# Routing and experts in one stage, with the blocks taken from both ends of the expert order

## The chip, the cores and the metric

The kernel runs on one core of one Trainium2 chip. The metric is the device time of one execution in microseconds (us). Three executions of the kernel before took 3208.84, 3212.40 and 3218.40 us; the median is 3212.4 us.

## The reference

Two transformer blocks follow each other, on 1024 tokens of width 1024 (S and D), in float32. Each ends with a mixture of experts: 16 experts in the first block, 32 in the second, in 4 groups. For every token:

```
grp    = argmax(group_logits)                 # 1 of 4 groups
e_in   = expert_logits[grp]                   # 4 or 8 logits of that group
top2   = top_k(e_in, 2)
weight = softmax(group_logits)[grp] * softmax over the two chosen
y      = sum over the two: weight * (silu(x @ w_gate[e]) * (x @ w_up[e])) @ w_down[e]
```

w_gate and w_up of an expert are 1024 x 256, w_down is 256 x 1024: 3 MB per expert. Everything ahead of the experts (projections, convolution or recurrence, attention, the output projection and the router's logits) is not touched.

## The kernel before

The program is a row of stages. Each stage owns its memory and semaphores, and `stage` clears the semaphores and makes all engines meet (line 116) when it ends. Within a stage each engine has its own instruction stream and its own queue; the engines meet at semaphores. `Steps` (called `own`) makes an engine wait for its own last instruction before it goes on. DMAs come from the queue of SP (weights, rows of the end) and from that of POOL (gathers and scatters by a list of rows).

`moe` (line 2423) runs two stages for each transformer block:

1. `route_tokens` (line 1402). VectorE (DVE) finds the group and the two experts of each token by comparisons over [128 tokens, 8 tiles, experts] tables. TensorE counts tokens by two products, one with a strict triangle (rank within a tile) and one with ones (totals). VectorE lays the experts' tokens out in blocks of 128, each block of one expert, and builds one-hot tables of place in the block and of block; 16 TensorE products turn them into a list of tokens per block (lines 1464, 1526 to 1563). Results are `token`, `choice`, `weights`, `expert` (of each block) and `passes`.
2. `run_experts` (line 1567 on). It walks the blocks in pairs p = 0, 1; `passes` says how often. SP reads the expert of a block from `expert` and loads its weights in three parts j = 0, 1 (1 MB each, halves of w_gate and w_up) and 2 (1 MB, w_down) into `raw[p][j]` (lines 1639 to 1651). ACT rounds them to a high part (`round_up`, `round_down`), VectorE subtracts to get the low part (`rest`, line 1867); each product is then three matmuls (high by high, high by low, low by high). POOL gathers the block's rows of v into `x[p]` (line 1679), TensorE turns them (line 1727), ACT and VectorE split them into `xT_high` and `xT_low`. TensorE makes the up products in two halves (line 1741), ACT and VectorE the gated middle, TensorE the down products (line 134), ACT copies them, and POOL scatters them (line 1691). At the end all rows are added up with their weights (line 1916).

A part's memory is given free one by one: SP loads `raw[p][j]` again once its low part is made; ACT rounds again once the products that read the high part are done. SP's loads, POOL's gathers and each engine's steps are in a fixed order written by hand. Before the loop ("first") the order of TensorE is: turn of block 0, turn of block 1, both up halves of block 0. In the list of blocks, slot n is block n. The experts of slots 0 and 1 are known to SP only from `expert`.

## Time and profile before

| | |
|---|---|
| median of 3 executions | 3212.4 us |
| profiled execution | 3206.69 us, span 3205.0 us |
| busy in the span | TensorE 85%, VectorE 49%, ACT 34%, POOL 25% |
| DMA | 405.00 MB, mean 126 GB/s |
| first expert part (routing, loop, end) | from about 1046 us |
| second expert part | from about 2753 us to the end |

The profile is of one execution. Busy time of an engine is the sum of its instructions; TensorE's clock is given as the granted share of full speed (0.50 or 1.00 within short stretches). Times in the rows are us from the start of the span.

### The profile page before, as it was taken

How to read it: one execution, taken by the hardware profiler on the slowest of the kernel's cores; microseconds unless marked ns; L12 is line 12 of the kernel's file. 1: busy time of each engine (PE TensorE's matmuls, PEld its weight loads, DVE VectorE, ACT ScalarE, POOL GpSimd, SP SyncE). 2: the span in 40 equal slices, each digit the busy share in tenths (PEclk: the TensorE clock that was granted, in tenths of full speed). 3: DMA queues.
4: the chain of work that ended last, by engine and by line, in shares of the span. 5: the costliest groups of instructions: out<-in, count | busy, mean ns of one | idle time of the engine just before them, and what ended most of it. 6: DMA issues, size and time to landing. Idle time of an engine off the chain costs nothing. (4 is left out here: it accounts for less than half of the span.)

```text
span 3205.0 us, 34426 instructions
## 1 busy us (share of the span) xinstructions
PE 2713.2 (85%) x11986; PEld 2022.5 (63%) x11986; DVE 1571.7 (49%) x1875; ACT 1085.8 (34%) x1435; POOL 798.1 (25%) x719
## 2 busy tenths in 40 slices
PE   5898897999979599719899699988999979499994
PEld 3897555767758477617655355556767757477773
DVE  4294341222232678661166444433643563487776
ACT  3012331000011377530133344431332131177773
POOL 1232331221211134302000233313322312034442
PEclk8999798999989699959799799998999989699997
DMA  2110112111132599853222232322111113299998
GB/s 88 34 46 24 31 33 55 53 39 39 33 119 99 215 345 361 324 187 129 114 59 60 69 78 78 80 53 68 40 39 46 46 49 144 110 345 335 343 326 323
DMA packets 237637, 405.00 MB, mean 126 GB/s; under 512 B 43512, under 2 KB 162632, under 8 KB 229608
## 3 DMA queue, kind: packets, MB, share of 16 engines
q1 hardware_dynamic: 220264, 370.21, 34.8%
q0 software_dynamic: 17280, 33.59, 2.7%
q8 instruction: 53, 0.87, 0.1%
q14 instruction: 40, 0.33, 0.0%
HBM read 351.97 MB, written 76.68 MB: 134 GB/s over the span
## 5 line engine op out<-in xcount | busy, mean ns | idle before, releaser
L1867 DVE TENSOR_TENSOR moe_run_w_low<-moe_run_w,moe_run_w_high 128x2048 fp32r<-128x2048 f32 x174 | 397.2, 2285 | 119.1 <-ACT moe_run_w_high L1793 108.9
L1793 ACT CAST moe_run_w_high<-moe_run_w 128x2048 fp32r<-128x2048 f32 x116 | 221.2, 1909 | 145.0 <-DMA moe_run_w<-w_up 66.4
L134 PE MATMUL rnn_ps<-uT_again_high,rnn_w_high 128*128 128x512 f32 x512 | 205.2, 401 | 36.1 <-POOL rnn_w_low L147 20.0
L134 PE MATMUL rnn_ps<-uT_again_low,rnn_w_high 128*128 128x512 f32 x512 | 202.5, 396 | 0.0
L134 PE MATMUL rnn_ps<-uT_again_high,rnn_w_low 128*128 128x512 f32 x512 | 202.3, 395 | 0.0
L1741 PE MATMUL moe_run_up<-moe_run_w_high,moe_run_xT_high 128*128 128x512 f32 x464 | 190.4, 410 | 0.3 <-DVE moe_run_w_low L1867 0.3
L134 PE MATMUL merge_gates<-uT_high,merge_wg_high 128*128 128x512 f32 x384 | 170.8, 445 | 17.4 <-POOL merge_wg_low L147 17.4
L1741 PE MATMUL moe_run_up<-moe_run_w_low,moe_run_xT_high 128*128 128x512 f32 x464 | 184.5, 398 | 0.0
L1741 PE MATMUL moe_run_up<-moe_run_w_high,moe_run_xT_low 128*128 128x512 f32 x464 | 184.3, 397 | 0.0
L1200 DVE TENSOR_TENSOR merge_gated<-merge_branch,merge_gate 128x512 f32<-128x512 f32 x48 | 33.2, 691 | 303.9 <-ACT merge_gate L1185 303.9
L1048 ACT ACTIVATE mla_probs<-mla_scores 128x512 f32<-128x512 f32 x192 | 94.2, 490 | 194.2 <-PE mla_scores L985 139.1
L1076 DVE TENSOR_REDUCE mla_piece_max<-mla_max 128x1 f32<-128x512 f32 (+1 forms) x192 | 100.7, 553 | 110.0 <-PE mla_max L960 71.0
L998 PE MATMUL mla_out<-mla_probs,mla_v 128*65 128x512 f32 (+3 forms) x384 | 153.6, 496 | 0.0
L134 PE MATMUL merge_gates<-uT_low,merge_wg_high 128*128 128x512 f32 x384 | 152.8, 398 | 0.0
L134 PE MATMUL merge_gates<-uT_high,merge_wg_low 128*128 128x512 f32 x384 | 151.6, 395 | 0.0
L1185 ACT ACTIVATE merge_gate<-merge_gates 128x512 f32<-128x512 f32 x48 | 28.8, 600 | 353.9 <-PE merge_branch L122 353.9
L134 PE MATMUL moe_run_down<-moe_run_w_high,moe_run_hT_high 128*128 128x512 f32 x232 | 99.2, 428 | 48.1 <-issue 44.7
L122 PE MATMUL mla_scores<-mla_q_hi,mla_k_hi 97*128 97x512 f32 x192 | 119.6, 623 | 23.0 <-DMA mla_q_hi<-mla_neg_rows 23.0
L134 PEld LDWEIGHTS rnn_ps<-uT_again_high,rnn_w_high 128*128 128x128 f32 x512 | 98.4, 192 | 59.0 <-issue 21.2
L122 PE MATMUL qkv_acc<-qkv_wq,latents_then_oT 128*128 128x512 f32 x288 | 126.9, 600 | 0.0
L1688 POOL COPY moe_run_to<-moe_choice 128x1 uint32 x58 | 64.6, 1114 | 243.9 <-ACT moe_run_y L1825 243.9
L122 PE MATMUL merge_branch<-features,merge_wy 128*128 128x512 f32 x256 | 117.7, 592 | 0.0
(447 smaller groups left out, 6722.2 us busy)
## 6 DMA issues: line engine op xcount, KB each, us to landing
moe_run_w<-exp_w SPq DMA_DIRECT2D x96, 512.0 KB
moe_run_w<-w_gate SPq DMA_DIRECT2D x68, 512.0 KB
moe_run_w<-w_up SPq DMA_DIRECT2D x68, 512.0 KB
moe_run_w<-w_down SPq DMA_DIRECT2D x34, 1024.0 KB
moe_run_w<-exp_w SPq DMA_DIRECT2D x24, 1024.0 KB
rnn_raw<-w_in SPq DMA_DIRECT2D x32, 512.0 KB
merge_raw<-w_in SPq DMA_DIRECT2D x24, 512.0 KB
moe_run_w_high<-moe_y SPq DMA_DIRECT2D x24, 512.0 KB, 8.0
```

What stands on the lines that cost most here:

```text
L122: last = pe.matmul(out, lhsT, rhs, start=(n == 0), stop=(n == len(pairs) - 1))
L134: last = pe.matmul(out, a, b, start=(k == 0), stop=(k == n - 1))
L998: pe.matmul(ps_o[n][0:DH + 1, first - a:b - a], v_aug[h % 2][0:rows, t, :], probs[g % R_P][0:rows, first - a:b - a], start=(t == 0), stop= ...
L1048: act.activation(probs[g % R_P][0:rows, first - a:b - a], ps_s[g % R_S][0:rows, first - a:b - a], ACT.Exp).then_inc(s_exp, 1)
L1076: dve.tensor_reduce(pm[:, i, n:n + 1], ps_m[g % R_M][:, 0:b - a], AX.X, ALU.max).then_inc(s_mxfree, 1)
L1185: act.activation(sg[u % NB][:], ps_g[u % NB][:], ACT.Sigmoid).then_inc(s_sg, 1)
L1200: dve.tensor_tensor(pr[b][:], ps_y[b][:], sg[b][:], ALU.mult).then_inc(s_done, 1)
L1688: pool.tensor_copy(to[p][:], r["choice"][:, bass.ds(b, 1)]).then_inc(s_to, 1)
L1741: last = pe.matmul(up[p][:], a, w, start=(h == 0 and k == 0), stop=(h == 1 and k == 3 * HK - 1))
L1793: act.copy(hi[p][j][:], raw[p][j][:]).then_inc(s_hi[j], 1)
L1867: dve.tensor_tensor(lo[p][j][:], raw[p][j][:], hi[p][j][:].bitcast(F32), ALU.subtract).then_inc(s_lo[j], 1)
```

## The change

`route_tokens` is gone and its steps are part of `run_experts`. In the new stage:

- A block's slot is no longer its number. With B blocks and half = B/2 rounded up, the block b < half has slot 2b, the others have slot 2B - 1 - 2b. Slot 0 is the first block of expert 0, slot 1 the last block of the last expert. So that this holds, every expert gets at least one block.
- SP loads the weights of expert 0 and of the last expert at the begin of the stage, by constants, and then waits for `expert`.
- ACT rounds five of these six parts ahead of the rest; POOL makes the first two low parts (`s_pre`), VectorE the others after the lists.
- POOL makes the tables' casts and clears x, and gathers the first two blocks' rows straight by `token`.
- The routing steps on VectorE are fewer and partly wider (both choices at once); the expert of each slot is found on one partition per slot and turned by a product. The weights' steps come after the loop.
- TensorE's order at the start is: turn of block 0, both up halves of block 0, turn of block 1.
- The routing's tables share memory with `g`, `squares` and `xT[1]`.

Core of the diff (declarations and the old routing, which the listing above shows, are left out):

```diff
+                def load(p, j, e):
+                    if j < 2:
+                        for n, w in enumerate(ups):
+                            sp.dma_start(raw[p][j][:, n], w[:, e, HK * j:HK * (j + 1), :]
+                                         .rearrange("p a c n -> p (a c) n")).then_inc(s_raw[p][j], 16)
+                    else:
+                        sp.dma_start(raw[p][j][:], dn[:, e].rearrange("p a c n -> p (a c) n")).then_inc(s_raw[p][j], 16)
+                def expert_of(i, p):
+                    return bass.ds(sp.value_load(expert[0:1, bass.ds(2 * i + p, 1)], min_val=0, max_val=E - 1), 1)
+                for p in range(2):
                     for j in range(3):
-                        if not first:
-                            sp.wait_ge(s_lo[j], 2 * i + p - 1)
-                        if j < 2:
-                            for n, w in enumerate(ups):
-                                sp.dma_start(raw[p][j][:, n], w[:, bass.ds(e, 1), HK * j:HK * (j + 1), :]
-                                             .rearrange("p a c n -> p (a c) n")).then_inc(s_raw[p][j], 16)
+                        load(p, j, slice(p * (E - 1), p * (E - 1) + 1))
+                sp.wait_ge(s_list, 1)
+                for p in range(2):
+                    e = expert_of(1, p)
+                    for j in range(3):
+                        if p == 0 and j < 2:
+                            sp.wait_ge(s_pre[j], 1)
                         else:
-                            sp.dma_start(raw[p][j][:], dn[:, bass.ds(e, 1)]
-                                         .rearrange("p a c n -> p (a c) n")).then_inc(s_raw[p][j], 16)
-                in_order(sp, load)
+                            sp.wait_ge(s_lo[j], p + 1)
+                        load(p, j, e)
                 n = more(sp)
+                with sp.Fori(1, n) as i:
+                    for p in range(2):
+                        e = expert_of(i + 1, p)
+                        for j in range(3):
+                            sp.wait_ge(s_lo[j], 2 * i + p + 1)
+                            load(p, j, e)
...
-                pool.iota(g_int[:], pattern=[[-1, NG]], base=NG, channel_multiplier=0)
-                pool.iota(t_int[:], pattern=[[P, NT]], base=0, channel_multiplier=1)
-                pool.iota(b_int[:], pattern=[[1, NB]], base=0, channel_multiplier=0)
-                own(pool.memset(strict[:], 1.0))
-                own(pool.affine_select(out=strict[:], in_=strict[:], compare_op=ALU.is_gt, fill=0.0, base=0,
-                                       pattern=[[1, P]], channel_multiplier=-1))
-                pool.sem_inc(s_const, 1)
-            @block.tensor
-            def _(pe):
-                pe.wait_ge(s_both, 1)
-                pe.wait_ge(s_const, 1)
-                flat = both[:].rearrange("p t e -> p (t e)")
-                pe.matmul(ps_rank[:, 0:NT * E], strict[:], flat, start=True, stop=True).then_inc(s_rank, 1)
-                pe.matmul(ps_tot[:, 0:NT * E], cst["ones"][:], flat, start=True, stop=True).then_inc(s_rank, 1)
-                for k in range(2):
-                    pe.wait_ge(s_hot, k + 1)
-                    for t in range(NT):
-                        last = pe.matmul(ps_id[:, 0:NB], in_block[k][:, t, :], of_block[k][:, t, :],
-                                         start=(k == 0 and t == 0), stop=(k == 1 and t == NT - 1))
-                last.then_inc(s_ids, 1)
-            @block.scalar
-            def _(act):
-                act.wait_ge(s_exp, 1)
-                act.activation(gx[:], gx[:], ACT.Exp).then_inc(s_exp, 1)
-                act.wait_ge(s_exp, 3)
-                act.activation(ex[:], ex[:], ACT.Exp).then_inc(s_exp, 1)
-            @block.vector
-            def _(dve):
-                own = Steps(dve, st.sem("dve_step"))
-                TT, TS = dve.tensor_tensor, dve.tensor_scalar
-                def wide(ap, n):
-                    return ap[:, :, None].broadcast_to((P, NT, n))
-                def table(ap, n):
-                    return ap[:, None, :].broadcast_to((P, NT, n))
-                def best(src, n, desc, onehot, t, out):
-                    own(dve.tensor_reduce(out[:], src, AX.X, ALU.max))
-                    own(TT(t, src, wide(out[:], n), ALU.is_equal))
-                    own(TT(t, t, table(desc[:], n), ALU.mult))
-                    own(dve.tensor_reduce(top[:], t, AX.X, ALU.max))
-                    own(TT(onehot[:], table(desc[:], n), wide(top[:], n), ALU.is_equal))
-                own(dve.memset(ones_e[:], 1.0))
-                dve.wait_ge(s_const, 1)
-                for a, b in ((e_desc, e_int), (g_desc, g_int), (t_id, t_int), (b_id, b_int),
-                             (p_id, p_int)):
-                    own(dve.tensor_copy(a[:], b[:]))
-                g, e = logits[:, :, 0:NG], logits[:, :, NG:NG + E]
-                best(g, NG, g_desc, goh, gpen[:], gmax)
-                TT(gx[:], g, wide(gmax[:], NG), ALU.subtract).then_inc(s_exp, 1)
-                own(TS(gpen[:], goh[:], BIG, -BIG, ALU.mult, ALU.add))
-                four = em[:].rearrange("p t (g e) -> p t g e", g=NG)
-                own(TT(four, e.rearrange("p t (g e) -> p t g e", g=NG),
-                       goh[:][:, :, :, None].broadcast_to((P, NT, NG, EG)), ALU.mult))
-                own(TT(four, four, gpen[:][:, :, :, None].broadcast_to((P, NT, NG, EG)), ALU.add))
-                best(em[:], E, e_desc, oh1, t3[:], v1)
-                own(TS(t3[:], oh1[:], -1e5 * BIG, None, ALU.mult))
-                own(TT(em[:], em[:], t3[:], ALU.add))
-                best(em[:], E, e_desc, oh2, t3[:], v2)
-                TT(both[:], oh1[:], oh2[:], ALU.add).then_inc(s_both, 1)
-                dve.wait_ge(s_exp, 2)
-                TT(ex[:], v2[:], v1[:], ALU.subtract).then_inc(s_exp, 1)
-                own(dve.tensor_reduce(tmp[:], gx[:], AX.X, ALU.add))
-                own(dve.reciprocal(gw[:], tmp[:]))
-                dve.wait_ge(s_exp, 4)
-                own(TS(tmp[:], ex[:], 1.0, None, ALU.add))
-                own(dve.reciprocal(tmp[:], tmp[:]))
-                own(TT(r["weights"][:, 0, :], gw[:], tmp[:], ALU.mult))
-                own(TT(r["weights"][:, 1, :], r["weights"][:, 0, :], ex[:], ALU.mult))
-                dve.wait_ge(s_rank, 2)
-                tot = ps_tot[:, 0:NT * E].rearrange("p (t e) -> p t e", t=NT)
-                own(dve.tensor_reduce(count[:], tot.rearrange("p t e -> p e t"), AX.X, ALU.add))
-                own(TS(count[:], count[:], 1.0 / P, (P - 1.0) / (2 * P), ALU.mult, ALU.add))
-                own(TS(nb[:], count[:], ROUND, ROUND, ALU.add, ALU.subtract))
-                own(dve.tensor_tensor_scan(ends[:], ones_e[:], nb[:], 0.0, ALU.mult, ALU.add))
-                own(TT(nb[:], ends[:], nb[:], ALU.subtract))
-                own(TS(place[:, 0, :], nb[:], float(P), None, ALU.mult))
-                for t in range(1, NT):
-                    own(TT(place[:, t, :], place[:, t - 1, :], tot[:, t - 1, :], ALU.add))
-                own(TT(place[:], place[:], ps_rank[:, 0:NT * E].rearrange("p (t e) -> p t e", t=NT), ALU.add))
-                for k, oh in enumerate((oh1, oh2)):
-                    own(TT(t3[:], oh[:], place[:], ALU.mult))
-                    own(dve.tensor_reduce(sl[:], t3[:], AX.X, ALU.add))
-                    own(TS(blk[:], sl[:], 1.0 / P, -(P - 1.0) / (2 * P), ALU.mult, ALU.add))
-                    own(TS(blk[:], blk[:], ROUND, ROUND, ALU.add, ALU.subtract))
-                    own(dve.scalar_tensor_tensor(out=pos[:], in0=blk[:], scalar=-float(P), in1=sl[:],
-                                                 op0=ALU.mult, op1=ALU.add))
-                    own(TT(in_block[k][:], table(p_id[:], P), wide(pos[:], P), ALU.is_equal))
-                    own(TT(of_block[k][:], table(b_id[:], NB), wide(blk[:], NB), ALU.is_equal))
-                    own(TS(sl[:], t_id[:], (k - 2.0) * S, None, ALU.add))
-                    TT(of_block[k][:], of_block[k][:].bitcast(F32), wide(sl[:], NB), ALU.mult).then_inc(s_hot, 1)
-                    dve.wait_ge(s_hot, k + 1)
-                own(TT(cmp[:], ends[0:1, None, :].broadcast_to((1, NB, E)),
-                       b_id[0:1, :, None].broadcast_to((1, NB, E)), ALU.is_le))
-                own(dve.tensor_reduce(be[:], cmp[:], AX.X, ALU.add))
-                own(TS(be[:], be[:], E - 1.0, None, ALU.min))
-                own(dve.tensor_copy(r["expert"][:], be[:]))
-                own(TS(pf[:], ends[0:1, E - 1:E], 0.5, 0.25, ALU.mult, ALU.add))
-                own(TS(pf[:], pf[:], ROUND, ROUND, ALU.add, ALU.subtract))
-                own(TS(pf[:], pf[:], 1.0, None, ALU.subtract))
-                own(dve.tensor_copy(r["passes"][:], pf[:]))
-                own(dve.memset(r["token"][:, NB:], S))
-                dve.wait_ge(s_ids, 1)
-                own(TS(choice[:], ps_id[:, 0:NB], 2.0 * S, None, ALU.add))
-                own(dve.tensor_copy(r["choice"][:], choice[:]))
-                own(TS(second[:], choice[:], float(S), -float(S), ALU.is_ge, ALU.mult))
-                own(TT(choice[:], choice[:], second[:], ALU.add))
-                dve.tensor_copy(r["token"][:, 0:NB], choice[:])
-def run_experts(nc, cst, name, experts, w1, w3, w2, v_d, y_d, r, h_d, g_row, out_d):
-    NB = block_count(experts)
     KH = HID // P
     HK = KD // 2
+    BIG = 1e30
     with stage(nc, name) as st:
         shape = [[P, 2, HK, HID], [P, 2, HK, HID], [P, KH, D]]
         raw, hi, lo = ([[st.sb(f"w{n}{j}_{p}", shape[j], dt) for j in range(3)] for p in range(2)]
@@ -1583,8 +1426,34 @@
         xT = [[st.sb(f"xT_{n}{p}", [P, KD, P], F32R) for n in ("high", "low")] for p in range(2)]
         sil, he = st.sb("silu", [P, HID]), st.sb("h", [P, HID])
         hT = [st.sb(f"hT_{n}", [P, KH, P], F32R) for n in ("high", "low")]
-        g, junk = st.sb("g", [P, D]), st.sb("squares", [P, D])
+        tail = st.sb("tail", [P, 2 * D])
+        g, junk = tail[:, 0:D], tail[:, D:2 * D]
         ss, ms, rt, inv = (st.sb(n, [P, NT]) for n in ("sums", "mean", "root", "inverse"))
+        weights = st.sb("weights", [P, 2, NT])
+        token, choice = st.sb("token", [P, NB + 2], U32), st.sb("choice", [P, NB], U32)
+        passes, expert = st.sb("passes", [1, 1], I32), st.sb("expert", [1, NB], I32)
+        e_int, g_int = st.sb("e_int", [P, E], I32), st.sb("g_int", [P, NG], I32)
+        t_int, b_int = st.sb("t_int", [P, 2, NT], I32), st.sb("b_int", [P, NB], I32)
+        p_int, s_int = st.sb("p_int", [P, P], I32), st.sb("s_int", [P, 1], I32)
+        e_desc, g_desc = st.sb("e_desc", [P, E]), st.sb("g_desc", [P, NG])
+        t_val, b_id, p_id = st.sb("t_val", [P, 2, NT]), st.sb("b_id", [P, NB]), st.sb("p_id", [P, P])
+        s_id, odd, along = st.sb("s_id", [P, 1]), st.sb("odd", [P, 1]), st.sb("along", [P, 1])
+        strict, keep = st.sb("strict", [P, P]), st.sb("keep", [P, E, NT])
+        gx, goh, gpen = (st.sb(n, [P, NT, NG]) for n in ("gx", "goh", "gpen"))
+        top, tmp, gmax, v1, v2, gw, ex = (st.sb(n, [P, NT]) for n in ("top", "tmp", "gmax", "v1", "v2", "gw", "ex"))
+        count, nb, ends, ones_e, below = (st.sb(n, [P, E]) for n in ("count", "nb", "ends", "ones_e", "below"))
+        half, last2, sb_at, sb_e = (st.sb(n, [P, 1]) for n in ("half", "twice_less_one", "block_at", "block_expert"))
+        at, blk, slot, pos = (st.sb(n, [P, 2, NT]) for n in ("at", "blk", "slot", "pos"))
+        second = st.sb("second", [P, NB])
+        def in_tail(n0, k):
+            return tail[:, n0 * NT * E:(n0 + k) * NT * E].rearrange("p (k t e) -> p k t e", k=k, t=NT)
+        t3, oh = in_tail(0, 2), in_tail(2, 2)
+        em, both, place = (in_tail(n, 1)[:, 0] for n in (4, 5, 6))
+        in_block = [t[:] for t in xT[1]]
+        of_block = [st.sb(f"of_block{k}", [P, NT, NB], F32R) for k in range(2)]
         def rows_of(tiles):
@@ -1595,13 +1464,22 @@
         yk = [parts[2 * t:2 * t + 2] for t in range(NT)]
         turn, hturn = st.ps("turn", (P, D)), st.ps("hturn")
         up, down = st.banks("up", 2), st.ps("down", (P, D))
+        ps_rank, ps_tot, ps_row, ps_id = down[:, 0:NT * E], down[:, BANK:BANK + NT * E], up[1], st.ps("ids")
+        s_tables, s_const = st.sem("tables_ready"), st.sem("constants_ready")
+        s_diff, s_exp = st.sem("differences_ready"), st.sem("exponents_ready")
+        s_both, s_rank = st.sem("choices_ready"), st.sem("ranks_ready")
+        s_hot, s_ids = st.sem("one_hots_ready"), st.sem("ids_ready")
+        s_bcol, s_brow = st.sem("block_experts_ready"), st.sem("block_experts_turned")
+        s_token, s_list = st.sem("tokens_ready"), st.sem("lists_ready")
+        s_pre = st.sem_n("first_low_ready")
         s_raw = [[st.sem(f"w{j}_loaded{p}") for j in range(3)] for p in range(2)]
         s_hi = [st.sem(f"w{j}_high_ready") for j in range(3)]
         s_lo = [st.sem(f"w{j}_low_ready") for j in range(3)]
         s_idx = st.sem("idx_ready")
         s_go = st.sem("may_go_on")
-        s_clear, s_to = st.sem("rows_cleared"), st.sem("to_ready")
+        s_to = st.sem("to_ready")
         s_h, s_yk = st.sem_n("h_loaded", NT), st.sem_n("choices_loaded", NT)
         s_g, s_sum = st.sem("g_loaded"), st.sem("summed")
         s_ss, s_ms, s_rt, s_inv, s_out = (st.sem(n) for n in ("sum_ready", "mean_ready", "root_ready",
@@ -1620,15 +1498,7 @@
         DOWN0, Y0 = 2, 1
         def more(eng):
-            return eng.value_load(r["passes"][0:1, 0:1], min_val=1, max_val=NB // 2 - 1)
-        def in_order(eng, body):
-            for p in range(2):
-                body(0, p, True)
-            with eng.Fori(0, more(eng)) as i:
-                for p in range(2):
-                    body(i + 1, p, False)
+            return eng.value_load(passes[0:1, 0:1], min_val=E // 2 - 1, max_val=NB // 2 - 1)
         with nc.Block() as block:
             @block.sync
@@ -1636,22 +1506,38 @@
                 ups = [w.rearrange("e (p c) n -> p e c n", p=P) for w in (w1, w3)]
                 dn = w2.rearrange("e (p c) n -> p e c n", p=P)
-                def load(i, p, first):
-                    e = sp.value_load(r["expert"][0:1, bass.ds(2 * i + p, 1)], min_val=0, max_val=experts - 1)
+                def load(p, j, e):
+                    if j < 2:
+                        for n, w in enumerate(ups):
+                            sp.dma_start(raw[p][j][:, n], w[:, e, HK * j:HK * (j + 1), :]
+                                         .rearrange("p a c n -> p (a c) n")).then_inc(s_raw[p][j], 16)
+                    else:
+                        sp.dma_start(raw[p][j][:], dn[:, e].rearrange("p a c n -> p (a c) n")).then_inc(s_raw[p][j], 16)
+                def expert_of(i, p):
+                    return bass.ds(sp.value_load(expert[0:1, bass.ds(2 * i + p, 1)], min_val=0, max_val=E - 1), 1)
+                for p in range(2):
                     for j in range(3):
-                        if not first:
-                            sp.wait_ge(s_lo[j], 2 * i + p - 1)
-                        if j < 2:
-                            for n, w in enumerate(ups):
-                                sp.dma_start(raw[p][j][:, n], w[:, bass.ds(e, 1), HK * j:HK * (j + 1), :]
-                                             .rearrange("p a c n -> p (a c) n")).then_inc(s_raw[p][j], 16)
+                        load(p, j, slice(p * (E - 1), p * (E - 1) + 1))
+                sp.wait_ge(s_list, 1)
+                for p in range(2):
+                    e = expert_of(1, p)
+                    for j in range(3):
+                        if p == 0 and j < 2:
+                            sp.wait_ge(s_pre[j], 1)
                         else:
-                            sp.dma_start(raw[p][j][:], dn[:, bass.ds(e, 1)]
-                                         .rearrange("p a c n -> p (a c) n")).then_inc(s_raw[p][j], 16)
-                in_order(sp, load)
+                            sp.wait_ge(s_lo[j], p + 1)
+                        load(p, j, e)
                 n = more(sp)
+                with sp.Fori(1, n) as i:
+                    for p in range(2):
+                        e = expert_of(i + 1, p)
+                        for j in range(3):
+                            sp.wait_ge(s_lo[j], 2 * i + p + 1)
+                            load(p, j, e)
                 if g_row is not None:
-                    sp.dma_start(g[:], g_row.to_broadcast((P, D))).then_inc(s_g, 16)
+                    sp.dma_start(g, g_row.to_broadcast((P, D))).then_inc(s_g, 16)
                 for t in range(NT):
                     if t % 2 == 0:
                         sp.wait_ge(s_lo[t // 2 % 2], 2 * n + 1 + t // 4)
@@ -1660,8 +1546,8 @@
                     sp.wait_ge(s_st[p], 16 * n + 16)
                 for t in range(NT):
                     for k in range(2):
-                        at = k * S + t * P
-                        sp.dma_start(yk[t][k], y_d[at:at + P, :]).then_inc(s_yk[t], 16)
+                        at0 = k * S + t * P
+                        sp.dma_start(yk[t][k], y_d[at0:at0 + P, :]).then_inc(s_yk[t], 16)
                 for t in range(NT):
                     if g_row is not None:
                         sp.wait_ge(s_out, t + 1)
@@ -1672,9 +1558,34 @@
             @block.gpsimd
             def _(pool):
+                own = Steps(pool, st.sem("pool_step"))
+                pool.iota(g_int[:], pattern=[[-1, NG]], base=NG, channel_multiplier=0)
+                pool.iota(e_int[:], pattern=[[-1, E]], base=E, channel_multiplier=0)
+                pool.iota(s_int[:], pattern=[[0, 1]], base=0, channel_multiplier=1)
+                pool.iota(t_int[:], pattern=[[S, 2], [P, NT]], base=-2 * S, channel_multiplier=1)
+                pool.iota(b_int[:], pattern=[[1, NB]], base=0, channel_multiplier=0)
+                pool.iota(p_int[:], pattern=[[1, P]], base=0, channel_multiplier=0)
+                pool.memset(ones_e[:], 1.0)
+                pool.memset(keep[:], 1.0)
+                own(pool.memset(strict[:], 1.0))
+                for f, n in ((g_desc, g_int), (e_desc, e_int)):
+                    pool.tensor_copy(f[:], n[:]).then_inc(s_tables, 1)
+                pool.affine_select(out=strict[:], in_=strict[:], compare_op=ALU.is_gt, fill=0.0, base=0,
+                                   pattern=[[1, P]], channel_multiplier=-1).then_inc(s_const, 1)
+                pool.memset(keep[:, :, 0:1], 0.0).then_inc(s_const, 1)
+                for f, n in ((t_val, t_int), (b_id, b_int), (p_id, p_int), (s_id, s_int)):
+                    pool.tensor_copy(f[:], n[:]).then_inc(s_const, 1)
+                for p in range(2):
+                    own(pool.memset(x[p][:], 0.0))
+                for j in range(2):
+                    pool.wait_ge(s_hi[j], 1)
+                    pool.tensor_tensor(lo[0][j][:], raw[0][j][:], hi[0][j][:].bitcast(F32),
+                                       ALU.subtract).then_inc(s_pre[j], 1)
...
-                pool.wait_ge(s_clear, 2)
-                gather(0, 0)
-                gather(1, 1)
+                pool.wait_ge(s_token, 1)
+                pool.sem_inc(s_go, 1)
+                for p in range(2):
+                    pool.indirect_dma_start(
+                        out=x[p][:], out_offset=None, in_=v_d,
+                        in_offset=bass.IndirectOffsetOnAxis(ap=token[:, p:p + 1], axis=0),
+                        bounds_check=S - 1, oob_is_err=False).then_inc(s_x[p], 16)
                 for p in range(2):
                     pool.wait_ge(s_turn, p + 1)
                     pool.sem_inc(s_go, 1)
                     gather(2 + p, p)
+                pool.wait_ge(s_list, 1)
...
+                pe.wait_ge(s_both, 1)
+                pe.wait_ge(s_const, 1)
+                flat = both.rearrange("p t e -> p (t e)")
+                pe.matmul(ps_tot, cst["ones"][:], flat, start=True, stop=True).then_inc(s_rank, 1)
+                pe.matmul(ps_rank, strict[:], flat, start=True, stop=True).then_inc(s_rank, 1)
+                for k in range(2):
+                    pe.wait_ge(s_hot, k + 1)
+                    for t in range(NT):
+                        last = pe.matmul(ps_id[:, 0:NB], in_block[k][:, t, :], of_block[k][:, t, :],
+                                         start=(k == 0 and t == 0), stop=(k == 1 and t == NT - 1))
+                last.then_inc(s_ids, 1)
+                pe.wait_ge(s_bcol, 1)
+                pe.matmul(ps_row[0:1, 0:NB], sb_e[0:NB, :], cst["ident"][0:NB, 0:NB], start=True,
+                          stop=True).then_inc(s_brow, 1)
...
                 turn_rows(0, 0, True)
-                turn_rows(0, 1, True)
                 up_half(0, 0, 0, True)
                 up_half(0, 0, 1, True)
+                turn_rows(0, 1, True)
+                pe.wait_ge(s_list, 1)
...
-                round_up(0, 0, 0, True)
+                for p in range(2):
+                    for j in range(2):
+                        round_up(0, p, j, True)
+                    if p == 0:
+                        round_down(0, 0, True)
+                act.wait_ge(s_diff, 1)
+                act.activation(gx[:], gx[:], ACT.Exp).then_inc(s_exp, 1)
+                act.activation(ex[:], ex[:], ACT.Exp).then_inc(s_exp, 1)
                 round_rows(0, 0, True)
-                round_up(0, 0, 1, True)
                 round_rows(0, 1, True)
-                round_up(0, 1, 0, True)
-                round_up(0, 1, 1, True)
-                round_down(0, 0, True)
                 gate(0, 0, True)
+                act.wait_ge(s_list, 1)
...
+                lg, le = logits[:, :, 0:NG], logits[:, :, NG:NG + E]
+                best(lg, NG, g_desc, goh[:], gpen[:], gmax, 1)
+                own(TS(gpen[:], goh[:], BIG, -BIG, ALU.mult, ALU.add))
+                own(TT(em.rearrange("p t (g e) -> p t g e", g=NG), le.rearrange("p t (g e) -> p t g e", g=NG),
+                       gpen[:][:, :, :, None].broadcast_to((P, NT, NG, EG)), ALU.add))
+                best(em, E, e_desc, oh[:, 0], t3[:, 0], v1, 2)
+                own(STT(out=em, in0=oh[:, 0], scalar=-1e5 * BIG, in1=em, op0=ALU.mult, op1=ALU.add))
+                best(em, E, e_desc, oh[:, 1], t3[:, 0], v2, 2)
+                TT(both, oh[:, 0], oh[:, 1], ALU.add).then_inc(s_both, 1)
+                own(dve.tensor_reduce(odd[:], cst["ident"][:].rearrange("p (c two) -> p two c", two=2)[:, 1, :], AX.X,
+                                      ALU.add))
+                dve.wait_ge(s_const, 6)
+                own(TS(along[:], odd[:], -1.0, 0.5, ALU.mult, ALU.add))
+                own(TT(along[:], along[:], s_id[:], ALU.mult))
+                own(STT(out=along[:], in0=odd[:], scalar=-0.5, in1=along[:], op0=ALU.mult, op1=ALU.add))
+                dve.wait_ge(s_rank, 1)
+                tot = ps_tot.rearrange("p (t e) -> p t e", t=NT)
+                by_e = t3[:, 0].rearrange("p t e -> p (t e)").rearrange("p (e t) -> p e t", t=NT)
+                dve.tensor_copy(by_e[:, :, 1:NT], tot.rearrange("p t e -> p e t")[:, :, 0:NT - 1])
+                own(dve.tensor_reduce(count[:], tot.rearrange("p t e -> p e t"), AX.X, ALU.add))
+                own(TS(count[:], count[:], 1.0, 1.0 / P, ALU.max, ALU.mult))
+                own(TS(count[:], count[:], (P - 1.0) / (2 * P), None, ALU.add))
+                own(TS(nb[:], count[:], ROUND, ROUND, ALU.add, ALU.subtract))
+                own(dve.tensor_tensor_scan(ends[:], ones_e[:], nb[:], 0.0, ALU.mult, ALU.add))
+                own(TT(nb[:], ends[:], nb[:], ALU.subtract))
+                own(TS(by_e[:, :, 0:1], nb[:][:, :, None], float(P), None, ALU.mult))
+                place_e = t3[:, 1].rearrange("p t e -> p (t e)")
+                own(dve.tensor_tensor_scan(place_e, keep[:].rearrange("p e t -> p (e t)"),
+                                           t3[:, 0].rearrange("p t e -> p (t e)"), 0.0, ALU.mult, ALU.add))
+                dve.wait_ge(s_rank, 2)
+                own(TT(place, place_e.rearrange("p (e t) -> p t e", t=NT),
+                       ps_rank.rearrange("p (t e) -> p t e", t=NT), ALU.add))
+                own(TT(t3, oh, place[:, None, :, :].broadcast_to((P, 2, NT, E)), ALU.mult))
+                blocks = ends[:, E - 1:E]
+                TS(half[:], blocks, 0.5, 0.25, ALU.mult, ALU.add)
+                TS(last2[:], blocks, 2.0, -1.0, ALU.mult, ALU.add)
+                own(dve.tensor_reduce(at[:], t3, AX.X, ALU.add))
+                own(TS(half[:], half[:], ROUND, ROUND, ALU.add, ALU.subtract))
+                own(TS(blk[:], at[:], 1.0 / P, -(P - 1.0) / (2 * P), ALU.mult, ALU.add))
+                own(TS(blk[:], blk[:], ROUND, ROUND, ALU.add, ALU.subtract))
+                own(STT(out=pos[:], in0=blk[:], scalar=-float(P), in1=at[:], op0=ALU.mult, op1=ALU.add))
+                own(TS(slot[:], blk[:], -4.0, last2[:], ALU.mult, ALU.add))
+                own(STT(out=slot[:], in0=blk[:], scalar=half[:], in1=slot[:], op0=ALU.is_ge, op1=ALU.mult))
+                own(STT(out=slot[:], in0=blk[:], scalar=2.0, in1=slot[:], op0=ALU.mult, op1=ALU.add))
+                for k in range(2):
+                    own(TT(of_block[k][:], table(b_id[:], NB), wide(slot[:, k], NB), ALU.is_equal))
+                    TT(in_block[k], table(p_id[:], P), wide(pos[:, k], P), ALU.is_equal)
+                    own(TT(of_block[k][:], of_block[k][:].bitcast(F32), wide(t_val[:, k], NB), ALU.mult))
+                    dve.sem_inc(s_hot, 1)
+                own(STT(out=sb_at[:], in0=odd[:], scalar=blocks, in1=along[:], op0=ALU.mult, op1=ALU.add))
+                own(TS(below[:], ends[:], sb_at[:], None, ALU.is_le))
+                own(dve.tensor_reduce(sb_e[:], below[:], AX.X, ALU.add))
+                TS(sb_e[:], sb_e[:], E - 1.0, None, ALU.min).then_inc(s_bcol, 1)
+                TS(passes[:], half[0:1, :], 1.0, None, ALU.subtract)
+                own(dve.memset(token[:, NB:], S))
+                dve.wait_ge(s_ids, 1)
+                own(TS(second[:], ps_id[:, 0:NB], -float(S), -float(S), ALU.is_ge, ALU.mult))
+                own(STT(out=token[:, 0:NB], in0=ps_id[:, 0:NB], scalar=2.0 * S, in1=second[:], op0=ALU.add, op1=ALU.add))
+                dve.sem_inc(s_token, 1)
+                own(TS(choice[:], ps_id[:, 0:NB], 2.0 * S, None, ALU.add))
+                dve.wait_ge(s_brow, 1)
+                own(dve.tensor_copy(expert[:], ps_row[0:1, 0:NB]))
+                dve.sem_inc(s_list, 1)
...
-                for p in range(2):
-                    dve.memset(x[p][:], 0.0).then_inc(s_clear, 1)
+                rest(0, 1, 0)
+                TT(ex[:], v2[:], v1[:], ALU.subtract)
+                TT(gx[:], lg, wide(gmax[:], NG), ALU.subtract).then_inc(s_diff, 1)
+                rest(0, 0, 2)
                 rest_of_rows(0, 0)
-                rest(0, 0, 0)
-                rest(0, 0, 1)
+                rest(0, 1, 1)
                 rest_of_rows(0, 1)
-                rest(0, 1, 0)
-                rest(0, 1, 1)
-                rest(0, 0, 2)
                 gated(0, 0, True)
...
+                dve.wait_ge(s_exp, 2)
+                own(dve.tensor_reduce(tmp[:], gx[:], AX.X, ALU.add))
+                own(dve.reciprocal(gw[:], tmp[:]))
+                own(TS(tmp[:], ex[:], 1.0, None, ALU.add))
+                own(dve.reciprocal(tmp[:], tmp[:]))
+                own(TT(weights[:, 0, :], gw[:], tmp[:], ALU.mult))
+                own(TT(weights[:, 1, :], weights[:, 0, :], ex[:], ALU.mult))
```

## Rows read from the trace of the kernel before

**Rows 1.** Stretches: us, busy (instructions) of each engine, PEclk, DMA share, GB/s
```profile
1046.00:1072.00 26.00, 5.00 (x20) 4.49 (x20) 20.63 (x82) 1.72 (x3) 1.03 (x7) 0.50 0.00 1
1072.00:1091.00 19.00, 3.92 (x16) 3.15 (x16) 4.67 (x4) 4.71 (x3) 3.82 (x6) 0.50 0.92 350
...
1120.00:1240.00 120.00, 110.25 (x511) 89.24 (x510) 94.59 (x68) 89.32 (x78) 49.56 (x44) 0.97 0.96 354
...
2850.00:3000.00 150.00, 137.52 (x643) 111.56 (x641) 118.47 (x85) 111.72 (x97) 67.35 (x57) 0.98 0.93 337
```

**Rows 2.** Timeline of DVE, first routing: start, us, engine, line, out<-in
```profile
1046.52 0.07 DVE L1494 MEMSET moe_route_ones_e<- 128x16 f32 x1 [0.95 <-PEq L116]
...
1054.73 0.29 DVE L1512 TENSOR_TENSOR moe_route_both<-moe_route_oh 128x128 f32<-128x128 f32 x1
...
1056.73 0.17 DVE L1527 TENSOR_SCALAR moe_route_count<-moe_route_count 128x16 f32<-128x16 f32 x1
...
1060.80 1.22 DVE L1542 TENSOR_TENSOR moe_route_in_block<-moe_route_p_id,moe_route_pos 128x1024 fp32r<-128x1024 f32 x1
...
1070.36 0.18 DVE L1563 CAST moe_token<-moe_route_choice 128x32 uint32<-128x32 f32 x1
```

**Rows 3.** Timeline of DVE, second routing
```profile
2753.14 0.09 DVE L1494 MEMSET moe_route_ones_e<- 128x32 f32 x1 [0.96 <-PEq L116]
...
2763.19 0.43 DVE L1512 TENSOR_TENSOR moe_route_both<-moe_route_oh 128x256 f32<-128x256 f32 x1
...
2783.52 0.19 DVE L1563 CAST moe_token<-moe_route_choice 128x48 uint32<-128x48 f32 x1
```

**Rows 4.** Timelines of SP, ACT, POOL, PE and DVE, start of both expert stages
```profile
1072.22 1.97 SPq L1646 DMA_DIRECT2D moe_run_w<-exp_w  x4
...
1079.06 1.90 ACT L1793 CAST moe_run_w_high<-moe_run_w 128x2048 fp32r<-128x2048 f32 x1 [23.71 <-DMA moe_run_w<-exp_w]
...
1074.75 1.21 POOL L1679 DMA_INDIRECT moe_run_x<-v,moe_run_idx  x1 [0.99 <-POOL moe_run_idx L1676]
...
1084.62 1.97 PE L1727 MATMUL moe_run_turn<-all_ident,moe_run_x 128*128 128x128 f32 x8 [15.89 <-DMA moe_run_x<-v,moe_run_idx]
...
1087.67 1.23 DVE L1873 TENSOR_TENSOR moe_run_xT_low<-moe_run_turn,moe_run_xT_high 128x1024 fp32r<-128x1024 f32 x1 [14.17 <-ACT moe_run_xT_high L1807]
1088.82 4.48 DVE L1867 TENSOR_TENSOR moe_run_w_low<-moe_run_w,moe_run_w_high 128x2048 fp32r<-128x2048 f32 x2
...
1091.15 0.80 PE L1741 MATMUL moe_run_up<-moe_run_w_high,moe_run_xT_high 128*128 128x512 f32 x1 [0.16 <-DVE moe_run_w_low L1867]
...
2787.88 1.09 POOL L1679 DMA_INDIRECT moe_run_x<-v,moe_run_idx  x1 [0.94 <-POOL moe_run_idx L1676]
...
2803.79 0.79 PE L1741 MATMUL moe_run_up<-moe_run_w_high,moe_run_xT_high 128*128 128x512 f32 x1 [0.17 <-DVE moe_run_w_low L1867]
```

**Rows 5.** Groups of POOL (count, busy, mean ns), then POOL's and DVE's timelines at 914
```profile
L147 POOL TENSOR_TENSOR merge_wg_low<-merge_raw,merge_wg_high 128x1024 fp32r<-128x1024 f32 x24 | 57.5, 2397 | 1.9
...
914.30 2.66 POOL L147 TENSOR_TENSOR out_merged_low<-features,out_merged_high 128x1024 fp32r<-128x1024 f32 x1
...
914.80 3.25 DVE L147 TENSOR_TENSOR out_merged_low<-features,out_merged_high 128x1024 fp32r<-128x1024 f32 x1
918.57 1.23 DVE L1346 TENSOR_TENSOR out_w_low<-out_raw,out_w_high 128x1024 fp32r<-128x1024 f32 x1 [0.52 <-ACT out_w_high L1378]
```

**Rows 6.** Timelines of POOL and DVE, a gather beside weight remainders
```profile
1094.19 1.02 POOL L1679 DMA_INDIRECT moe_run_x<-v,moe_run_idx  x1 [0.85 <-POOL moe_run_idx L1676]
...
1094.35 6.69 DVE L1867 TENSOR_TENSOR moe_run_w_low<-moe_run_w,moe_run_w_high 128x2048 fp32r<-128x2048 f32 x3
```

**Rows 7.** Chain of waits at the end: start, us, what
```profile
3168.47 2.08 DMA moe_y<-moe_run_y,moe_run_to
```

**Rows 8.** Timeline of ACT, silu of slots 1 and 22
```profile
1105.64 0.39 ACT L1814 ACTIVATE moe_run_silu<-moe_run_up 128x256 f32<-128x256 f32 x1
...
1333.35 0.39 ACT L1814 ACTIVATE moe_run_silu<-moe_run_up 128x256 f32<-128x256 f32 x1
```

## Prediction of the time after

> **What bounds the kernel now.** I read the table of stretches first, because only the two expert parts are touched. While tokens are routed the DMA share is zero and VectorE works in small steps. In the next 19 us DMA runs at 0.92 and TensorE does 3.9 us of work. In the passes that follow DMA stands at 0.93 to 0.96 and TensorE is busy 110 of 120 us [rows 1]. So inside an expert part there are two regimes: a serial start that nothing hides, and a loop in which weights stream at nearly the full rate of the queues. The loop's pace comes from the silu rows: slot 1 at 1105.64, slot 22 at 1333.35, so 227.7 / 21 = 10.84 us a block [rows 8].
>
> Then the timelines of the two starts. In the first part VectorE's routing runs from 1046.52 to 1070.54, 24.0 us, and in the second from 2753.14 to 2783.71, 30.6 us [rows 2, 3]. After it come the stage's end, the clearing of x and the first gather's issue at 1074.75, 4.2 us later (4.2 at 2787.88 too). From that issue to the first up product it takes 16.4 us (1091.15) and 15.9 us (2803.79). Within it the gathered rows are late: issued at 1074.75, turned at 1084.62, 9.9 us, with 6 MB of weights in the queues. The low half of the rows ends at 1088.90, and the low half of the weights holds the product until 1091.15 [rows 4]. That is the point to note: weights that come earlier remove only 2.2 us of waiting by themselves; the rest must come from the gather and the routing.
>
> **The change part by part.** All sums are against the profiled execution (3206.7 us, span 3205.0), 5.7 us under the median 3212.4; I subtract the gain from the median.
>
> *Routing chain.* Each VectorE step that waits for its predecessor costs its duration plus 0.04: 0.21 us at up to 32 elements, 0.33 at 128, 0.46 at 256, 1.26 at 1024, about 0.70 at 512 between the last two [rows 2, 3]. Removed from the chain, first part / second part: the five table casts and two steps that now run while POOL makes the tables, 1.4 / 1.4; the multiplication of expert logits, 0.33 / 0.46; a scaling folded into the next step, 0.26 / 0.33; the order of the two rank products and the weights moved behind the loop, 0.4 / 1.0; seven row sums (0.21 each, 1.5) against a scan and a copy, 0.8 / 0.6; the second one-hot's own slot arithmetic done together with the first, 0.4 / 0.4; the comparison of all blocks with all experts, done on one partition over blocks x experts elements, now spread over the partitions and beside the last products, 1.3 / 3.5. A new step for empty experts costs 0.2. Sum 4.7 / 7.5 us; the token list is ready after 19.3 us and 23.1 us. Between ends: nothing to 7 / 10, since the new wide steps are not in the trace. Counting the seeds' inputs through the reference gives 23 and 33 blocks and no empty expert, so the number of slots (24 and 34) stays.
>
> *From list to gather.* Now 4.2 us; after, no stage end and no clearing on the way, the gather reads the list directly, and one wait before a gather costs 0.99 us (the idle time in the row at 1074.75 [rows 4]). Saved 3.2 us, twice.
>
> *Gather to first product.* The nearest rows for the landing: 9.9 us with 6 MB queued [rows 4], 2.08 us for a scatter into empty queues [rows 7]. After the change the first weights have landed and 2 MB of slot 2's are issued at about the same moment, so I take 5.0 and keep both ends. From turned rows to their low half 1084.62 to 1088.90, 4.3 us, and 0.1 to the product. 9.4 against 16.4 / 15.9: saved 7.0 / 6.5. VectorE has by then done two of the three weight remainders between list and rows, 2 x 2.24 us [rows 4], and this fits in the 9 us it waits. ACT's five roundings and the exponents lie beside routing: the first pair of weights lands 6.8 us after its issue (1072.22 to 1079.06), all six within some 18 us, less than routing.
>
> *Two remainders on POOL, while VectorE routes.* This is the part that costs. POOL needs 2.40 us for 128x1024, so 4.7 to 4.8 for each of the two 128x2048 [rows 5]. The first high half is ready 6.8 + 1.9 = 8.7 us after the stage begins; POOL then works until about 18.2 us, within both routing chains. The rows at 914 show what VectorE does meanwhile: POOL's subtraction runs 914.30 to 916.96, VectorE's own starts at 914.80 and takes 3.25 us, where the same shape takes 1.23 alone at 918.57. It ends 1.1 us after POOL's: it stood still until POOL had finished [rows 5]. The routing chain is serial, nearly all its steps read two SBUF operands, so one blocked step holds all. Price 2 x 4.7 = 9.4 us for each part, 18.8 in all. Bounds: 0 if small steps slip through, 13 for each part if POOL's wait for VectorE is added (2.66 instead of 2.40 and more).
>
> The Trainium skill speaks of this in SBUF — State Buffer, section SBUF: two separate sides: the port pair shared by the two engines is an exclusive lock for a whole instruction, and a VectorE step with one SBUF input outside the two-port modes does not need it. By that rule the reductions and the copies from PSUM run on, at most one or two in each of POOL's instructions, and the stall would be about 18 us instead of 18.8. The row at 914 agrees on the block; no row shows a small step beside POOL.
>
> The same section warns that a gather issued by POOL cannot write its descriptors while VectorE runs a two-port instruction. Here VectorE starts a remainder right after the list. In this trace the gather at 1094.19 takes 1.02 us though VectorE is in its remainders from 1094.35 [rows 6], so I charge nothing; by the warning read broadly it would be up to 2.2 us for each part.
>
> *New order at the start.* Before, both slots' rows are turned before the first product, hidden under the wait. After, slot 1's rows are turned behind slot 0's two up halves. Then TensorE waits: a turn of 1.0 (1.97 at half clock, at full clock half of it) and, as between 1086.59 and 1088.90, 2.3 us for high and low half [rows 4]. 3.3 us lost, twice; from 0 if the slots' rest hides it. ACT's gate of slot 0 waits behind it too, but TensorE needs its result only after slot 1's first half.
>
> *What follows.* The weights of slots 2 and 3 no longer arrive just in time, and TensorE can go at its own pace of 110.25 x 10.84 / 120 = 10.0 us instead of 10.84 for two blocks [rows 1, 8]: 1.7 us, and at slot 4 a queue that is emptier by half of slot 3's second megabyte, 0.5 / 0.35 = 1.4 us at the 354 GB/s of [rows 1]. About 3.0 for each part; between 0 and 5. Not more, since slot 4's loads wait for slot 2's buffers to be rounded, and those for the first products: a load that is ready earlier cannot run further ahead than the ring. The loop itself is the same, so 10.84 stays.
>
> *Tail.* Six weight steps (1.3 us) lie behind the loop, where VectorE waits for the results' way through memory (2.08 us of scatter and the loads after it [rows 7]). No cost.
>
> Sum for the first and second part: 4.7 + 3.2 + 7.0 - 9.4 - 3.3 + 3.0 = 5.2 and 7.5 + 3.2 + 6.5 - 9.4 - 3.3 + 3.0 = 7.5. Together 12.7 us: 3206.7 - 12.7 = 3194.0 for a profiled execution, 3199.7 on the scale of the median.
>
> **The rivals.**
> A, no stall: the small steps run beside POOL. For it: they are 0.2 to 0.5 us long, and the only row on it has wide operands. Against: the row shows a full stop. Then the gain is 12.7 + 18.8 = 31.5, so 3181 us.
> B, the gathers are as slow as before: slot 2's and 3's weights are let go by the same routing result, and the rows land 9.9 us after issue instead of 5.0. For it: the trace never shows a gather in an empty queue. Against: only 2 MB are asked for at that moment, not 6. Gain 12.7 - 9.8 = 2.9: 3209.5 us.
> C, slower: the port is traded to and fro. If each of POOL's subtractions waits for VectorE's step, and is itself a third slower, as 3.25 us for 128x1024 would be (the time that the VectorE row at 914 shows for two in turn), each lasts 6.5, the stall is 13.0 instead of 9.4, the first gather starts after a later list and the lead for slots 2 and 3 is gone: 12.7 - 7.2 - 6.0 = -0.5, and with B's collision, which then comes at the same time, -10.3. So 3212.9 to 3222.7, in the middle 3218 us. It decides from a stall of 13 us a part on.
> D, the change does not do what it says: the first weights are not early, because the lists gate them. Not possible by the code, slot 0 and 1 take expert 0 and the last by constants; I give it nothing.
>
> **How the numbers follow.** 0.3% is 9.6 us, about what a measurement of this kernel can tell from no change. Forecast 0.58, A 0.24, B 0.10, C 0.08. In the forecast's own case the bounds give 3192 to 3207, and about 0.7 of it lies under 3202.8. Faster: 0.58 x 0.7 + 0.24 = 0.65; slower 0.07 of C; the rest, 0.28, is the same. The range goes from 3176, which takes in A, to 3210, which takes in B.
>
> **What would show it.** In the profile of the changed kernel: the first weights issued right at the stage's begin and DMA share near 0.9 in the first 18 us of it; the token list 29 us (first part) and 33 us (second) after the begin, with two stretches of some 4.7 us in which a VectorE step of 0.2 to 0.5 us takes long, each ending with a POOL subtraction; a gather landing 5 us after issue; the first up product at about 1085.6, and a gap of 3.3 us in TensorE behind its 24th product; the silu rows 10.8 us apart from slot 4 on. The prediction is wrong if the list is ready after 19 and 23 us (A), if the rows take 9 us again (B), or if the loop's pace changes: 0.1 us a block is 6 us in all.

## The result and the profile after

The change made the kernel slower. In the first comparison (20 executions each) the ratio of the time after to the time before is 1.0027, 95% interval [1.0015, 1.0040]: 8.6 us more. Timed again it was 1.0018 [1.0004, 1.0032]. Forecast was 12.7 us less, within a range of 3176 to 3210 us; the fastest of the 20 executions after took 3214.7 us. Some executions of every kernel are slow, by some 2%: ratios are of the fast ones alone, and the profiles of again (3262.54 us) and all_three (3241.40 us) are of slow ones, which lost their time ahead of the first expert part, so their moments within the parts are used. The profiled execution took 3225.47 us (span 3223.7); its first expert part begins 3 us later than before, from work that the change does not touch, so the moments in the table below are counted from the begin of each part (the first VectorE instruction of routing). Times in the rows are us from the start of the span, as before.

Stretches of the first part after, columns as in [rows 1]: early loads, end of routing, gathers, first products, loop.
```profile
1049.00:1067.00 18.00, 1.22 (x4) 0.93 (x4) 15.37 (x27) 7.86 (x5) 12.99 (x21) 0.50 0.90 336
1067.00:1079.00 12.00, 3.97 (x18) 3.65 (x18) 9.59 (x35) 2.92 (x2) 0.14 (x1) 0.50 0.05 22
1079.00:1094.00 15.00, 1.97 (x8) 1.57 (x8) 5.34 (x5) 1.34 (x3) 5.35 (x4) 0.50 0.87 303
1094.00:1121.00 27.00, 23.93 (x99) 19.58 (x100) 13.88 (x11) 12.96 (x12) 4.28 (x7) 0.83 0.34 103
1121.00:1240.00 119.00, 108.75 (x504) 88.08 (x503) 93.08 (x66) 86.99 (x76) 56.15 (x44) 0.97 0.97 355
```
The load does run beside routing now (0.90). But what follows is new: DMA stands nearly still for 12 us and again runs at 0.34 for the 27 us after 1094, where before it had 0.93 in the 27 us after its own first product (1091 to 1118). The loop looks as in [rows 1].

VectorE's steps for the list and the subtraction behind them, from its timeline in the kernel after (start, us, engine, line):
```profile
1058.29 0.28 DVE L1843 TENSOR_REDUCE moe_run_count<-moe_run_down 128x16 f32<-128x128 f32 x1
1058.61 4.09 DVE L1844 TENSOR_SCALAR moe_run_count<-moe_run_count 128x16 f32<-128x16 f32 x1
1062.73 4.44 DVE L1845 TENSOR_SCALAR moe_run_count<-moe_run_count 128x16 f32<-128x16 f32 x1
...
1078.07 0.19 DVE L1882 SCALAR_TENSOR_TENSOR moe_run_token<-moe_run_ids,moe_run_second 128x32 uint32<-128x32 f32 x1
...
1078.96 2.29 DVE L1891 TENSOR_TENSOR moe_run_w_low<-moe_run_w,moe_run_w_high 128x2048 fp32r<-128x2048 f32 x1
```
POOL's timeline in the same kernel, the two low halves and then the gathers:
```profile
1058.16 8.98 POOL L1583 TENSOR_TENSOR moe_run_w_low<-moe_run_w,moe_run_w_high 128x2048 fp32r<-128x2048 f32 x2 [4.26 <-ACT moe_run_w_high L1727]
1079.60 2.75 POOL L1610 DMA_INDIRECT moe_run_x<-v,moe_run_token  x1 [12.46 <-issue]
```
Two steps of 0.17 us last 4.09 and 4.44 us; the second ends at 1067.17, where POOL's second subtraction ends (1067.14). The reduction that reads PSUM at 1058.29 passes. And the gather takes 2.75 us where it took 1.21 in [rows 4]: VectorE's subtraction began 0.64 us before it, and the gather's instruction ends 1.1 us after that subtraction (1082.35 against 1081.25).

In the second part it is the same, with other steps in the way. POOL's second subtraction there, then VectorE's steps beside it:
```profile
2778.64 4.71 POOL L1583 TENSOR_TENSOR moe_run_w_low<-moe_run_w,moe_run_w_high 128x2048 fp32r<-128x2048 f32 x1
2778.90 0.21 DVE L1832 TENSOR_REDUCE moe_run_odd<-all_ident 128x1 f32<-128x64 f32 x1
2779.14 0.15 DVE L1836 TENSOR_SCALAR moe_run_along<-moe_run_odd 128x1 f32<-128x1 f32 x1
2779.33 4.04 DVE L1837 TENSOR_TENSOR moe_run_along<-moe_run_along,moe_run_s_id 128x1 f32<-128x1 f32 x1
```
A reduction and a one-element step with a single SBUF input pass, and a one-element step with two of them waits until POOL ends (2783.37 against 2783.35).

TensorE's timeline in the kernel after, the turn of slot 0's rows and the first products:
```profile
1090.23 1.97 PE L1657 MATMUL moe_run_turn<-all_ident,moe_run_x 128*128 128x128 f32 x8 [12.32 <-DMA moe_run_x<-v,moe_run_token]
1094.66 0.77 PE L1674 MATMUL moe_run_up<-moe_run_w_high,moe_run_xT_high 128*128 128x512 f32 x1 [2.45 <-DVE moe_run_xT_low L1897]
...
1106.05 0.47 PE L1674 MATMUL moe_run_up<-moe_run_w_high,moe_run_xT_high 128*128 128x512 f32 x1 [2.41 <-issue]
```
Moments within a part, worked out from such rows, for all kernels (us from the part's begin; first part / second part). The rows count as landed when TensorE begins to turn them; "first up" is the first up product; the pace of the loop is from the silu of slot 1 to that of slot 21 in the first part and 31 in the second:

| kernel | ratio to before | list ready | rows after 1st gather | first up | slot 1's silu | loop, us a block |
|---|---|---|---|---|---|---|
| before | 1 | 24.0 / 30.6 | 9.9 / 9.4 | 44.6 / 50.7 | 59.1 / 65.1 | 10.87 / 10.73 |
| the change | 1.0027, 1.0018 | 28.4 / 32.0 | 10.6 / 11.1 | 44.8 / 48.5 | 64.8 / 69.1 | 11.02 / 10.81 |
| low_on_dve | 0.9963 | 20.3 / 24.9 | 10.0 / 8.4 | 35.7 / 38.8 | 55.8 / 59.3 | 10.88 / 10.81 |
| rows_first | 1.0002 | 28.5 / 32.0 | 5.8 / 6.1 | 40.1 / 43.5 | 59.8 / 64.2 | 10.99 / 10.86 |
| turn_first | 0.9992 | 28.2 / 33.1 | 10.8 / 10.9 | 46.3 / 51.1 | 59.7 / 65.5 | 10.92 / 10.89 |
| gather_alone | 1.0004 | 28.1 / 32.1 | 8.8 / 5.2 | 42.6 / 42.8 | 60.1 / 62.9 | 10.89 / 10.77 |
| plain_order | 1.0028 | 28.2 / 33.0 | 11.2 / 10.7 | 45.2 / 49.1 | 65.5 / 69.0 | 10.90 / 10.86 |
| late_loads | 1.0030 | 20.2 / 24.9 | 9.2 / 9.2 | 44.7 / 49.7 | 63.8 / 69.9 | 10.88 / 10.91 |
| all_three | 0.9935 | 20.3 / 24.9 | 6.5 / 6.4 | 33.8 / 38.4 | 48.1 / 52.3 | 10.92 / 10.90 |
| ring | 0.9746 | 20.3 / 24.9 | 6.4 / 6.2 | 33.8 / 38.1 | 48.0 / 52.3 | 9.51 / 9.93 |
| before_ring | 0.9831 | 24.0 / 30.6 | 9.8 / 9.2 | 44.5 / 50.5 | 59.0 / 65.1 | 9.51 / 9.86 |
| change_ring | 0.9845 | 28.5 / 32.0 | 10.8 / 10.3 | 45.0 / 47.7 | 62.4 / 65.6 | 9.52 / 9.87 |
| four_ring | 0.9755 | 20.2 / 24.6 | 4.9 / 4.1 | 33.7 / 37.7 | 48.0 / 52.2 | 9.51 / 9.84 |

With SP's old order of requests the total follows the start: what slot 1's silu gains or loses in the two parts together is within 4 us of what the total does (the change +9.7 us against +8.6, low_on_dve -9.1 against -12, turn_first +1.0 against -3, all_three -23.8 against -21).

### The profile page after: what moved, and what is told of

Read it like the earlier page. It is cut to its first block and busy times, and to the rows that moved or that the text cites. A ratio compares the mean times of both kernels' runs of the same rounds, so it can differ in the third digit from the quotient of the medians.

```text
span 3223.7 us, 34309 instructions
## 1 busy us (share of the span) xinstructions
PE 2722.0 (84%) x11990; PEld 2029.2 (63%) x11990; DVE 1572.5 (49%) x1841; ACT 1086.6 (34%) x1435; POOL 837.1 (26%) x743
## 5 line engine op out<-in xcount | busy, mean ns | idle before, releaser
L1891 DVE TENSOR_TENSOR moe_run_w_low<-moe_run_w,moe_run_w_high 128x2048 fp32r<-128x2048 f32 x170 | 388.7, 2286 | 125.2 <-ACT moe_run_w_high L1727 113.6
L134 PE MATMUL moe_run_down<-moe_run_w_high,moe_run_hT_high 128*128 128x512 f32 x232 | 99.1, 427 | 51.5 <-issue 48.1
L1599 POOL COPY moe_run_to<-moe_run_choice 128x1 uint32 x58 | 64.8, 1118 | 238.8 <-ACT moe_run_y L1759 238.8
L146 POOL CAST rnn_w_high<-rnn_raw 128x1024 fp32r<-128x1024 f32 x32 | 34.9, 1091 | 322.4 <-PE rnn_ps L134 274.2
```

Source lines behind the costliest of these rows:

```text
L134: last = pe.matmul(out, a, b, start=(k == 0), stop=(k == n - 1))
L146: own(eng.tensor_copy(high, raw))
L1599: pool.tensor_copy(to[p][:], choice[:, bass.ds(b, 1)]).then_inc(s_to, 1)
L1891: dve.tensor_tensor(lo[p][j][:], raw[p][j][:], hi[p][j][:].bitcast(F32), ALU.subtract).then_inc(s_lo[j], 1)
```

## The experiments

Each ratio is against the kernel before, timed on the same chip in five rounds. The edits are to the changed kernel unless said otherwise.

**low_on_dve.** The low halves go back to VectorE.
```diff
-                for j in range(2):
-                    pool.wait_ge(s_hi[j], 1)
-                    pool.tensor_tensor(lo[0][j][:], raw[0][j][:], ...).then_inc(s_pre[j], 1)
 # ... VectorE, after the lists:
+                for j in range(2):
+                    dve.wait_ge(s_hi[j], 1)
+                    dve.tensor_tensor(lo[0][j][:], raw[0][j][:], ...).then_inc(s_pre[j], 1)
                 rest(0, 0, 2)
+                rest(0, 1, 0)                 # moved here from ahead of the loop
                 rest_of_rows(0, 0)
```


> Undoes one part of the change: the low halves of slot 0's up weights are made by VectorE after the lists, not by POOL beside the routing. The change as it is takes 8.6 us more than before (ratio 1.0027). Theory P (VectorE stands still in the routing while POOL subtracts): the two long routing steps (4.1 and 4.4 us in the first part, 4.6 and 4.0 in the second) go back to under 0.5 us, the token list is ready 20.5 us (first) and 24.5 us (second) after the stage's begin instead of 28.7 and 32.3, and the whole is 16 us faster than the change: about 8 us under before. Rival: the list is earlier, but the gathered rows or the first weights are what is late, and under half of it arrives: at most 4 us faster than before.

Measured 0.9963 [0.9949, 0.9977], 12 us under before and 20 under the change. The list comes at 20.3 and 24.9 us; the step that took 4.09 us takes 0.17. All four subtractions fit into the time in which the rows are on their way:
```profile
1053.36 0.17 DVE L1839 TENSOR_SCALAR moe_run_count<-moe_run_count 128x16 f32<-128x16 f32 x1
...
1065.72 4.49 DVE L1911 TENSOR_TENSOR moe_run_w_low<-moe_run_w,moe_run_w_high 128x2048 fp32r<-128x2048 f32 x2
1070.13 4.49 DVE L1886 TENSOR_TENSOR moe_run_w_low<-moe_run_w,moe_run_w_high 128x2048 fp32r<-128x2048 f32 x2
1078.88 1.23 DVE L1892 TENSOR_TENSOR moe_run_xT_low<-moe_run_turn,moe_run_xT_high 128x1024 fp32r<-128x1024 f32 x1 [4.27 <-ACT moe_run_xT_high L1736]
```
Theory P holds, and the work that POOL had taken over cost nothing visible where it came from. The edit also moves SP's requests for slots 2 and 3: in the first part the last of the 4 MB is asked for 8.9 us after the first gather begins, against 5.2 in the change. The rows land 0.6 and 2.7 us sooner, and how much of this comes from the later requests no run separates.

**rows_first.**
```diff
                 sp.wait_ge(s_list, 1)
+                for p in range(2):
+                    sp.wait_ge(s_x[p], 16)
```


> SP asks for slot 2's weights only when the rows of slots 0 and 1 have landed; all else as in the change. Theory Q (the gathers share the queues with 4 MB of weights asked for at the same moment): the rows of slot 0 are there 5 to 6 us after the first gather begins instead of 10.6 and 11.1, the first up product comes 5 us earlier in each part, and as slot 4's weights are not asked for earlier than the first products allow, the delayed loads cost nothing: 10 us faster than the change, so 1 us under before. Theory R (the gather is slow because VectorE's subtractions delay POOL's descriptors): still 9 to 11 us, and the same time as the change or up to 10 us more, as slot 2's weights are late.

Measured 1.0002 [0.9990, 1.0014], some 8 us under the change. The gather instruction still takes 2.75 us, but the rows are there after 5.8 and 6.1 us. Timeline of POOL, then of TensorE:
```profile
1073.98 2.75 POOL L1612 DMA_INDIRECT moe_run_x<-v,moe_run_token  x1 [12.46 <-issue]
...
1079.79 1.97 PE L1659 MATMUL moe_run_turn<-all_ident,moe_run_x 128*128 128x128 f32 x8 [7.48 <-DMA moe_run_x<-v,moe_run_token]
```
So nearly half of the 10.6 us was the weights of slots 2 and 3, asked for from 0.3 us after the gather began (0.6 us in the second part).

**gather_alone.** VectorE waits until both gathers are issued.
```diff
+                pool.sem_inc(s_asked, 1)      # POOL, behind the two gathers
+                dve.wait_ge(s_asked, 1)       # VectorE, ahead of rest(0, 1, 0)
```


> VectorE begins its weight subtractions only after POOL has issued both first gathers. Theory R (VectorE's subtraction stretches the gather instruction from 1.0 to 2.8 and 3.0 us): both gather instructions take 1.0 to 1.1 us and slot 0's rows land 2 to 5 us earlier: 4 to 10 us faster than the change. Theory Q (the queues are shared with the weights): the instructions get short, but the rows land within 1 to 2 us of where they did: at most 3 us faster than the change.

Measured 1.0004 [0.9990, 1.0018], some 7 us under the change, which is in theory R's range. The first gather takes 1.23 us:
```profile
1072.39 1.23 POOL L1611 DMA_INDIRECT moe_run_x<-v,moe_run_token  x1 [12.45 <-issue]
1073.92 1.98 POOL L1611 DMA_INDIRECT moe_run_x<-v,moe_run_token  x1 [0.30 <-issue]
```
and rows land after 8.8 and 5.2 us: 1.8 us sooner in the first part, theory Q's size, and 5.9 in the second, more than R's. With rows_first this shows that both causes are real. Their gains do not add up (in the second part 5.0 and 5.9 us alone, 7.0 with both edits in four_ring), as if a gather written late found more weights ahead of it; that reason, and why the parts differ, no run isolates.

**turn_first.**
```diff
                 turn_rows(0, 0, True)
+                turn_rows(0, 1, True)
                 up_half(0, 0, 0, True)
                 up_half(0, 0, 1, True)
-                turn_rows(0, 1, True)
```


> TensorE turns slot 1's rows before slot 0's up products, as before the change. Theory T (the new order leaves TensorE idle for 2.4 us behind slot 0's products, and the granted clock, back at 0.5 for some 3.5 us after that gap, costs 2 us more): from the first up product to slot 1's silu it takes 14.5 us again instead of 19.9 and 20.6; the first up product itself comes 2 to 3 us later; net 2.5 us in each part, 5 us faster than the change. Rival: slot 1's rows land so late that turning them first holds the first product back by as much as it saves: no difference.

Measured 0.9992 [0.9980, 1.0003], some 11 us under the change. From first up to slot 1's silu it takes 13.4 and 14.4 us (20.0 and 20.6 in the change, 14.5 and 14.4 before); the first product comes 1.5 and 2.6 us later, so slot 1's silu gains 5.1 and 3.6 us. Right in kind, twice the size forecast.

**again.** The change once more, no edit.


> The change itself, unchanged, timed beside the others. Ratio to the kernel before 1.0027 as measured first (8.6 us more): between 1.001 and 1.004. In the profile: token list 28.4 and 32.0 us after the begin of the two parts, slot 0's rows 10.6 and 11.1 us after the first gather, slot 1's silu at 64.8 and 69.1 us (59.1 and 65.1 before).

1.0018 [1.0004, 1.0032]; list 28.7 and 32.0, rows 11.1 and 11.0, silu 65.7 and 69.1 us. The pattern repeats to a microsecond.

**plain_order.** Slot n is block n, slots 0 and 1 by constants.
```diff
-                        load(p, j, slice(p * (E - 1), p * (E - 1) + 1))
+                        load(p, j, slice(p, p + 1))
 # slot = blk; block of a slot = its number
```


> Slots in the old order (slot n is block n), with the experts of slots 0 and 1 as constants, which holds for these inputs; all else as in the change. In the four kernels so far the loop from slot 5's silu to the last takes 194 to 197 us in the first part and 298 to 303 in the second, before the change 192 and 297. Theory O (the order from both ends makes the weights' stream slower): the loop goes back to 192 and 297 and the kernel is 3 to 8 us faster than the change. Rival (the order does nothing): the same loop and the same total as the change within 3 us.

1.0028 [1.0014, 1.0042], as the change: the order does nothing that can be told, theory O falls. From slot 5's silu to the last it takes 195 and 301 us with the old order too.

**late_loads.** low_on_dve, and the first loads behind the list.
```diff
+                sp.wait_ge(s_list, 1)
                 for p in range(2):
                     for j in range(3):
                         load(p, j, slice(p * (E - 1), p * (E - 1) + 1))
-                sp.wait_ge(s_list, 1)
```


> Low halves on VectorE after the lists (ratio 0.9963), but SP asks for the first weights only when the lists are ready: routing and experts in one stage without the early load. Weights of five parts must then land (6.8 us for the first pair, 18 us for all) and be rounded by ACT before the rows, so slot 0's first product comes about 8 us later than with the early load, at 43 to 45 us and 47 to 49 us after the begin: 14 to 18 us in all, ratio 1.001 to 1.002. Rival (the early load itself is worth nothing, as the gathered rows are late anyway): within 4 us of 0.9963.

1.0030 [1.0018, 1.0041] against 0.9963: the early load is worth 21 us in this form, somewhat more than the 14 to 18 expected, and 9 and 11 us at the first product. In this version ACT's five roundings stand ahead of the rows, so part of this is ACT's order.

**all_three.** The edits of low_on_dve, rows_first and turn_first together.


> Low halves on VectorE after the lists, slot 2's weights asked for after the rows of slots 0 and 1 have landed, and slot 1's rows turned before slot 0's products, together. If the three costs are independent: list at 20.3 and 24.9 us, rows 6 us after the gather, slot 1's silu at 47 to 49 and 52 to 54 us, 11 us earlier in each part than before the change, and the whole 20 to 22 us under before: ratio 0.993 to 0.994. Rival (they overlap: the weights' stream, not the start, sets the loop's end): slot 1's silu is as early, but the total is that of the low halves alone, 0.9963.

0.9935 [0.9911, 0.9959], 21 us under before. Slot 1's silu comes 11.0 and 12.8 us earlier than before, 23.8 together, and nearly all of it is in the total.

**ring.** The same, with SP's requests in another order: the down weights of a slot are asked for behind the up weights of the next. The loop's part of the edit, comments added:
```diff
-                    for j in range(3):            # slot b: up, up, down
-                        sp.wait_ge(s_lo[j], 2 * i + p + 1)
-                        load(p, j, e)
+                ups_of(i + 1, 0, ...)             # slot b: up, up
+                down_of(i, 1, 2 * i)              # slot b - 1: down
+                ups_of(i + 1, 1, ...)
+                down_of(i + 1, 0, 2 * i + 1)
```


> As all three together, and SP asks for the up weights of a slot before the down weights of the slot before it. Theory S (a start that is earlier is not carried on, since SP stands before slot 3's down weights until slot 1's gate is done, with slot 4's up buffers already free; in the change DMA moves nothing for some 15 us there): slot 4's up weights are asked for 5 us earlier, DMA shows no such gap, slot 5's silu comes 2 to 4 us earlier in each part and the total is 4 to 8 us under that of the three together. Rival (the loop's pace is what the queues carry, 10.8 us a block, and the gap is made up for elsewhere): no difference within 3 us, or slower, as the down weights now come late for the down products.

0.9746 [0.9727, 0.9764], 81 us under before and 60 under all_three, ten times what I expected. Stretches of the loop, same columns:
```profile
1120.00:1240.00 120.00, 120.00 (x579) 99.57 (x578) 108.63 (x76) 103.41 (x89) 88.20 (x52) 1.00 1.02 406
```
TensorE is busy in 120 of 120 us and DMA moves 406 GB/s where [rows 1] has 354. A block takes 9.51 us; the prediction put TensorE's own pace at 10.0.

**before_ring.** The kernel before, with SP's new order and nothing else.


> The kernel before the change with one edit: SP asks for the up weights of a slot before the down weights of the slot before it (from slot 3 on). If the loop's pace of 10.84 us a block was never what the queues carry but SP's order, the pace goes to 9.5 to 10.0 us with no help from the change: 22 blocks x 1.2 and 32 x 0.9 us, 50 to 60 us in all, ratio 0.981 to 0.985. Rival (the pace needs the earlier start as well): pace between 10.4 and 10.84 and a ratio above 0.99.

0.9831 [0.9818, 0.9843], 54 us under before, as expected: the old pace was SP's order. Pace 9.51 and 9.86 us. SP's requests of its timeline:
```profile
1102.85 4.76 SPq L1645 DMA_DIRECT2D moe_run_w<-exp_w  x4
1109.35 0.33 SPq L1648 DMA_DIRECT2D moe_run_w<-exp_w  x1
1112.35 4.72 SPq L1645 DMA_DIRECT2D moe_run_w<-exp_w  x4
```
Both halves of the up weights and a down load every 9.5 us. In the kernel before, VectorE's and SP's timelines show the wait that is gone:
```profile
1105.77 2.29 DVE L1867 TENSOR_TENSOR moe_run_w_low<-moe_run_w,moe_run_w_high 128x2048 fp32r<-128x2048 f32 x1 [0.58 <-ACT moe_run_w_high L1793]
1108.32 2.28 DVE L1867 TENSOR_TENSOR moe_run_w_low<-moe_run_w,moe_run_w_high 128x2048 fp32r<-128x2048 f32 x1
...
1110.62 0.33 SPq L1649 DMA_DIRECT2D moe_run_w<-exp_w  x1
1112.29 1.89 SPq L1646 DMA_DIRECT2D moe_run_w<-exp_w  x4
```
The first subtraction is slot 2's second up half, which frees the last of slot 4's up buffers at 1108.06; the second is slot 1's down half, which frees the buffer of slot 3's down load at 1110.60. SP stands before that down load and asks for slot 4's up weights 4.2 us after their buffers are free.

**change_ring.** The change with SP's new order.


> The change with the same edit of SP's order. With a loop that TensorE sets, a late start is carried to the end as it is: slot 1's silu comes 5.7 and 4.0 us later than before the change (as measured), so the kernel is 8 to 12 us slower than the kernel before with that edit. Rival (once SP no longer holds back slot 4's loads, the early weights of slots 2 and 3 give the change its lead): 3 us or more faster than the kernel before with that edit.

0.9845 [0.9829, 0.9861] against 0.9831 on the same chip: 4.5 us slower, about half of the 8 to 12 expected, and the intervals overlap. Slot 1's silu is 3.4 and 0.5 us later than in before_ring, 3.9 together. The total again follows slot 1's silu; the change is not a gain there either.

**four_ring.** ring with gather_alone's edit.


> All three edits with SP's new order (ratio 0.9746), and VectorE begins its weight subtractions only after POOL has issued both first gathers. The first gather instruction goes from 3.2 to about 1.1 us. If the rows land that much earlier, and VectorE's four subtractions (9.1 us) still fit ahead of them, the start is 1 to 2 us earlier in each part: 2 to 4 us, ratio 0.9735 to 0.974. Rival: the subtractions then end after the rows have been turned and hold the low half of the rows back, so no difference or up to 4 us slower.

0.9755 [0.9739, 0.9770] against 0.9746 [0.9727, 0.9764] on another chip: no difference that can be told. The rival stated ahead came true: the rows land after 4.9 and 4.1 us, yet the first product stays at 33.7 us, since VectorE's subtractions end at 1075.12 and hold the low half of the rows until then (it begins at 1075.03, in ring at 1075.12). ring and four_ring are the fastest kernels of this study.

## Why the prediction was wrong

Up to slot 1's silu I had forecast 2.2 and 4.5 us of gain (5.2 and 7.5 less the lead of 3.0 each). Measured is a loss of 5.7 and 4.0 us. The difference, 16.4 us, lies in these steps (11.7 at the landing and 5.1 in the order, less 0.4 in the rest):

- *Gather to first product* failed. "I take 5.0" for the landing; it was 10.6 and 11.1, 11.7 us in all. The bound of 9.9 us was in the text, and rival B (0.10) was this mechanism. Two things were missed. Not 2 but 4 MB of loads are asked for within some 6 us, beginning 0.3 us (0.6 in the second part) behind the gather's begin, and rows_first shows that they cost about 5 us. And "I charge nothing" for VectorE beside the gather rested on a misread row: the gather at 1094.19 in [rows 6] had begun 0.16 us before VectorE's subtraction. In the change the subtraction begins first, and the instruction takes 2.75 and 3.01 us; gather_alone brings it to 1.23 and 1.1. SBUF — State Buffer of the Trainium skill, section SBUF: two separate sides, names a VectorE step with two SBUF inputs as one that shuts out a GpSimd step reading SBUF; the gather reads its list from SBUF, and these rows agree. The same section of the Trainium skill also says that such a step did not stall a DMA from GpSimd in a probe; for this gather the measurement goes the other way, and it decides. That it is the reading of the list that waits is argued, not shown.
- *New order at the start* was mis-sized: 3.3 us a part forecast. Between the first up product and slot 1's silu the change takes 5.5 and 6.2 us more than the kernel before, 5.1 more than forecast in all; turn_first takes that back, for a first product that is 1.5 and 2.6 us later. The gap of 2.4 us and the turn were in the sum. Not in it was the clock, twice. TensorE's granted clock was 1.00 before the gap and 0.50 (1.2 in place of 2.4 GHz) again for some 3.4 us behind it, beginning 0.4 and 1.0 us after the products had resumed: the ten products from 1106.05 take 3.96 us, where ten at 1.00 take 2.3, so 1.6 us, and 1.6 in the second part too. And slot 0's 24 products take 7.9 and 8.4 us where the kernel before, with slot 1's turn just ahead of them, needs 7.2 and 7.5: the clock rises only after about 12 and 14 of them instead of 7 and 9, which is 0.8 us a part. Windows of the kernel after, columns as in [rows 1]: the gap, the stretch at the half clock, and the full clock again.
```profile
1104.00:1105.00 1.00, 0.00 (x0) 0.00 (x0) 0.27 (x1) 0.98 (x2) 0.15 (x2) 1.00 0.00 0
1107.00:1108.00 1.00, 1.00 (x4) 0.71 (x4) 0.00 (x0) 1.00 (x1) 0.00 (x0) 0.50 0.81 283
1110.00:1111.00 1.00, 1.00 (x8) 0.91 (x7) 0.50 (x1) 0.10 (x1) 0.00 (x0) 1.00 0.00 0
```
A product of 128x512 lasts 0.63 us and the next begins 0.43 us after it at 0.50; at 1.00 it is 0.39 and 0.23. In turn_first, which has no such gap, the clock stays at 1.00 from 1090 to 1105 us, the same stage of the part.
- *Two remainders on POOL* held in kind. Forecast 9.4 a part; low_on_dve shows the list 8.1 and 7.1 us earlier, 3.6 us less in all. The blocked steps in the first part have a single SBUF input (128x16, TENSOR_SCALAR), in the second two, while the reduction from PSUM, a reduction from SBUF and a TENSOR_SCALAR of one element pass. The same section of the Trainium skill frees a step with one SBUF input only outside the two-port modes; the rows do not contradict it, but in which mode a step ran no run here shows. Rival A is refuted.
- *Routing chain* and *from list to gather* held: without the stall 20.3 and 24.9 us against 19.3 and 23.1 forecast, 2.8 us less saved in all, and the gather 1.3 and 1.0 us behind the list. That the list came at 28.4 and 32.0 us, close to the 29 and 33 of the prediction, is in part luck: the two misses of 3.6 and 2.8 us cancel.
- *What follows* failed in its reading of the loop. I took a DMA share of 0.93 to 0.96 and a pace of 10.84 us for a stream at the queues' limit, and let 3.0 us of lead be kept in each part. Nothing was kept: from slot 1's silu to the last one it takes 2 us longer in each part than before, in the profile of again 0.7 us longer and 0.4 us less. before_ring shows why the premise was false: the same bytes flow at 9.51 us a block in the first part once SP does not stand before a down load whose buffer frees late, with the next slot's up buffers already free. In the change this wait is longest at the start: slot 4's first up buffer is free at 1110.50 and asked for at 1121.50, behind slot 3's down load at 1119.56, and meanwhile DMA stands at 0.34. I had named the ring as a limit of the lead, but not seen that it set the whole loop.

The sum misses thus by 16.4 us in the start and by 6 us of lead that did not come: -12.7 + 22.4 is 9.7 us more, against 8.6 measured. The agreement should not be overrated: the two profiled executions themselves lie 18.8 us apart, 3.3 of it ahead of the first part and 4.3 behind slot 1's silu, which again does not repeat.

The number itself fell into the band of rival C (3212.9 to 3222.7 us, chance 0.08): 3212.4 and 8.6 are 3221.0. But C was to decide from a stall of 13 us a part on, and that did not come (8.1 and 7.1 us). What it shares with the result is rival B's collision at the gather and the lead that is gone. C named neither the longer gather instruction, the clock behind the gap nor SP's order.

What stays open: how the 10.6 us of the landing divide between the queues and the longer gather instruction (the two edits together were tried only with the other edits), and what sets the second part's 9.9 us a block in the new order, where the first has 9.51. From 2800 to 2950 us of ring TensorE is busy 143.25 of 150 us, with DMA at 0.99 and 367 GB/s.

## What to carry to other kernels

Before work is moved beside a serial chain, ask what it shares with the engines and queues of that chain: here 9 us of POOL work made the list of rows 7 to 8 us later, though VectorE had idle time a few steps behind it. A prefetch that is released by the same event as an urgent small transfer should wait for it. And a DMA share of 0.96 is no proof of a limit: look at what each load's issue waits for in the queue's own order, and change that order once before the loop is called bound by bandwidth.

## What the runs showed of the hardware

- A gather of 128 rows landed after 4.1 to 4.9 us with its instruction undisturbed and no loads beside it, 5.8 to 6.5 with VectorE subtracting beside it, 5.2 and 8.8 undisturbed but with 4 MB of loads asked for in the 6 us from its begin (gather_alone), and 10.6 to 11.2 with both (the change, again, turn_first and plain_order).
- A DMA share of 1.02 came with 406 GB/s (ring) and 0.96 to 0.97 with 353 to 355 (the kernels before and after): 6% in the share were 15% in the rate.
- Beside a POOL subtraction of 128x2048 (4.5 to 4.7 us) VectorE's small steps with two SBUF inputs, and one of 128x16 with a single one, waited until it ended; a reduction (0.21 us from SBUF, 0.28 from PSUM) and a one-element step with a single SBUF input (0.15 us) did not.
- A gap of 2.4 us in TensorE's products was followed by about 3.4 us at the half clock in both parts, beginning 0.4 and 1.0 us after the products resumed; it cost 1.6 us each time.
